# A sum moved behind a turn in neighbourhood attention, and eight copies moved from ScalarE to VectorE

## The chip, the cores and the metric

The kernel runs on one core of a Trainium2 chip. The metric is the device time of one execution, in microseconds. TensorE (PE in the rows) multiplies, VectorE (DVE) and ScalarE (ACT) compute element by element and can read PSUM, GpSimd (POOL) computes on SBUF, and SyncE (SP) issues transfers.

## The reference

Two blocks of a sequence model on 512 tokens of width 1024, all in fp32; the second block has two layers and 256 context tokens beside the 512. The diff touches one part: the attention over a neighbourhood in the even layer. Each of 8 heads of width 64 lets each of 512 queries attend to a window of tokens on a grid and to the 256 context tokens, with a table of biases; the 256 context queries attend to the context alone. The steps that matter, for a block of 128 queries and one head:

```
logits = q @ k.T + bias          # 128 x 256, 384 or 512
p = exp(logits - max(logits))
out = (p / sum(p)) @ v           # 128 x 64
```

## The kernel before, in words

The program is written out by hand for each engine; engines meet by semaphores, and each works off its own list in order. Attention is done in *pairs*: one block of 128 queries for two heads at once. Neighbourhood attention has 24 pairs, six for each of four pairs of heads (`na_pairs`): pairs 0 and 1 of six are the context's queries, which see 256 keys (2 blocks of 128 keys for each head, "short"), pairs 2 to 4 see 512 keys (4 blocks, "wide"), and pair 5 holds the two edges of the grid and sees 384 keys ("edge").

What one pair n goes through:

1. TensorE, `score`: logits of both heads into PSUM (L1083).
2. VectorE, `largest`, once for each head h: takes bias minus logits and its least value (L1193, L1201 for short pairs). It is called M(n,h) below.
3. ScalarE: exponential with its row sum, once for each head (L1161).
4. VectorE: reciprocal of the row sum (L1181); GpSimd: scales the probabilities by it (L1026).
5. TensorE, `turn`: transposes the probabilities into the PSUM banks 6 and 7 (L1101). It waits until they are scaled and until the copy of pair n-1 has emptied the two banks.
6. The copy of the turned probabilities to SBUF (L1149), by ScalarE for all 24 pairs.
7. TensorE, `sum`: probabilities times values (L1121). It waits for the copy.
8. VectorE, `store`: the result to SBUF (L1209).

All pairs of this stage are turned in one piece, the `closing` phase; `phases` says for each piece which engine copies it. The pairs run staggered. At step p of its loop, TensorE turns pair p-3, sums pair p-4 and scores pair p. VectorE's step p holds, in this order: a copy of pair p-3 if it is VectorE's, M(p,0), the reciprocals of pair p-1, the store of pair p-3, M(p,1), and then what `na_between_vector` adds: in steps 0 and 1 of each six the masking of the bias table, in steps 6, 9, 12 and 15 one "mix split" (L1272, a subtraction that prepares the next projection). ScalarE's step for pair p has the first exponential, the copy of pair p-2, the second exponential, and after pairs 5, 8, 11 and 14 a cast for a mix split (L1265). In steps 24 to 26 TensorE has matmuls of the next projection in place of scores.

Attention with grouped queries uses the same class later (stage `gqa`), with other arguments.

Of the kernel before, what the change touches and what calls it, by code (L numbers as in the profile page):

```python
# [19 lines left out]
T = S + CTX  # L20
# [90 lines left out]
class Serial:  # L111
# [3 lines left out]
    def __init__(self, eng, own):  # L115
        self.eng, self.own, self.n, self.at, self.per = eng, own, 0, None, 0
# [351 lines left out]
def wide_products(k, pe, times, bank=7):  # L468

    for _ in range(times):  # L470
        pe.matmul(k.bank(bank), k.h_hi[:, 0, 0:P], k.h_hi[:, 0, 0:S], start=True, stop=True)  # L471
# [173 lines left out]
class Projection:  # L645
# [21 lines left out]
    def tensor(self, pe, lo, ready=None, stored=None, done=0):  # L667
        k, n = self.k, self.tiles
        for i, events in enumerate(self.slots):
            if i < n:  # L670
                u = FIRST[self.name] + i
                size = self.jobs[i][0].shape[-1]
                widths = (S, size - S) if size > S else (S,)
                if i < SPLITS and ready is not None:
                    if i == 0:
                        first_units(k, pe, self.name, k.h_hi, lo, widths, ready)
                else:
                    if i == 1 and stored is not None:
                        pe.wait_ge(*stored)
                    if i >= 3:  # L680
                        pe.wait_ge(self.evac, self.e + i - 2)
                    if u not in HALVED:
                        pe.wait_ge(k.lo_done, u + 1)
                    unit_products(k, pe, 2 * (i % 3), u, k.h_hi, lo, DT, widths, at=(done if i == 0 else 0, DT))
            elif i < n + self.units:
                values_unit(k, pe, self.values, lo, T // P, self.width, i - n, self.units, (self.evac, self.e, n))
            for j in events:
                x, mean = self.jobs[j][0:2]
                size = x.shape[-1]
                pe.wait_ge(self.squares, self.b + j + 1)  # L690
                if j >= 1:
                    pe.wait_ge(self.rooted, self.b + j)
                last = pe.matmul(k.bank(6), mean, k.sq[:, j % 2, 0:S], start=True, stop=True)
                if size > S:
                    last = pe.matmul(k.bank(7, size - S), mean, k.sq[:, j % 2, S:size], start=True, stop=True)
                last.then_inc(self.summed, 1)
# [334 lines left out]
Phase = collections.namedtuple("Phase", "a b by turned kept copies")  # L1031


class RowTiledAttention(PairAttention):


    def __init__(self, k, pairs, third, before, opened, wide=(0, 0, 0), by=("act", "act")):
        super().__init__(k, pairs, third, before, opened, wide)
        count = dict(self.first)
        self.phases, kept = {}, (count["act"], count["dve"])  # L1040
        for p, it in enumerate(pairs):
            n = it["blocks"]
            self.phases[p] = []
            for which, a, b in [(1, 0, 2 * n)] if 2 * n <= TURNED else [(0, 0, n), (1, n, 2 * n)]:
                count["chunks"], count[by[which]] = count["chunks"] + 1, count[by[which]] + 1
                self.phases[p].append(Phase(a, b, by[which], count["chunks"], kept, (count["act"], count["dve"])))
                kept = (count["act"], count["dve"])
        self.last.update(count, pairs=self.last["pairs"], parted=self.last["parted"], mixed=self.last["mixed"], scaled=self.last["scaled"])

# [75 lines left out]
    def tensor(self, pe, begun=0, beside=None):  # L1125
        N = len(self.pairs)
        for p in range(N + 4):
            if p >= 4:
                self.sum(pe, p - 4)
            self.turn(pe, p - 3, self.closing(p - 3))  # L1130
            if begun <= p < N:
                self.score(pe, p)
            if p >= N and beside is not None:
                if p == N:
                    self.place_free(pe)
                beside(p - N)
            if p < 3:
                self.open(pe, "fill", p)
                wide_products(self.k, pe, self.fill[p])
            self.turn(pe, p - 2, self.opening(p - 2))  # L1140
# [513 lines left out]
def attn_views(k):  # L1654

    return (k.view(k.big, 0, 4, T), k.view(k.big, 4 * T, 4, T), k.view(k.big, 8 * T, 6, HALF))
# [7 lines left out]
def pair(q, keys, values, out, bias=None, factor=None):  # L1664

    chunks = [keys[:, a:min(a + CTX, keys.shape[-1])] for a in range(0, keys.shape[-1], CTX)]
    return pair_of([(slice(0, P), q, chunks)], [[(slice(0, P), val)] for val in values], out, bias, factor)


def pair_of(pieces, values, out, bias, factor=None):  # L1670

    return dict(pieces=pieces, ends=list(itertools.accumulate(ap.shape[-1] for ap in pieces[0][2])), n=len(values) * P, values=values,
                blocks=len(values), out=out, bias=bias, factor=factor, joined=factor is not None)
# [29 lines left out]
def na_table(k, t):  # L1703

    return k.view(k.mix_flat, 5 * T, 5, CTX) if t == 0 else k.view(k.big, 12 * T + 5 * CTX * t, 5, CTX)


def na_pairs(k):


    q, key, val = attn_views(k)
    out = []
    for t in range(4):
        vals, mix, table = [val[:, b, t * P:(t + 1) * P] for b in range(6)], k.mix[:, 4 + t, :], na_table(k, t)
        whole, ctx = [[(slice(0, P), v)] for v in vals], key[:, t, S:T]
        for i in (4, 5):
            blk = slice(i * P, (i + 1) * P)
            out.append(pair(q[:, t, blk], ctx, vals[4:], mix[:, blk], bias=[k.par("zero").broadcast_to([P, CTX])] * 2))
        for i in range(3):
            blk = slice(HD + i * P, HD + (i + 1) * P)  # L1720
            out.append(pair_of([(slice(0, P), q[:, t, blk], [key[:, t, i * P:i * P + CTX], ctx])], whole[i:i + 2] + whole[4:],
                               mix[:, blk], bias=[table[:, 0::3, :], table[:, 1:4:2, :]]))
        low, high, units = slice(0, HD), slice(HD, P), table.rearrange("p a (u n) -> p (a u) n", n=P)
        out.append(pair_of([(low, q[:, t, 0:HD], [key[:, t, 0:P], ctx]), (high, q[:, t, S - HD:S], [key[:, t, S - P:S], ctx])],
                           [[(low, vals[0]), (high, vals[3])]] + whole[4:],
                           mix[:, 0:S].rearrange("p (e n) -> p e n", n=HD)[:, ::S // HD - 1, :], bias=[units[:, 4:9:2, :], units[:, 5:10:2, :]]))
    return out
# [59 lines left out]
def gqa_pairs(k):  # L1787

    q, key, val = gqa_views(k)
    return [pair(q[:, t, i * P:(i + 1) * P], key[:, 0, 0:T], [val[:, b, :] for b in range(6)],  # L1790
                 k.mix[:, t, i * P:(i + 1) * P]) for t in range(4) for i in range(4)]


def pair_stages(k):

    first = {("score", 0): [("dil_project_evac", 8), ("values_kept_dve", 1), ("values_kept_act", 1)],
             ("score", 1): [("values_kept_dve", 2), ("values_kept_act", 2)]}
    dil = PairAttention(k, dil_pairs(k), k.big[:, 10240:10240 + 2 * S], None, first, (2, 2, 8))
    first = {("score", 0): [("head_normed", 16), ("values_kept_dve", 5), ("values_kept_act", 4)],
             ("score", 1): [("values_kept_act", 5)]}  # L1800
    diff = PairAttention(k, diff_pairs(k), k.mix_flat[:, 4 * T:6 * T], dil, first, (2, 8, 4))
    first = {("score", 0): [("head_normed", 24), ("head_rooted", 28), ("values_kept_act", 10)],
             ("score", 1): [("values_kept_act", 11)], ("turn", 0): [("head_normed", 28)]}
    na = RowTiledAttention(k, na_pairs(k), k.h_flat[:, 4 * T:6 * T], diff, first, (2, 2, 10))
    first = {("score", 0): [("head_normed", GQA + 2), ("gqa_evac", 5)], ("score", 1): [("gqa_evac", 6)],
             ("fill", 1): [("head_rooted", GQA + 5), ("head_normed", GQA + 5)]}
    first.update({("score", 4 * t): [("head_normed", GQA + 2 + t)] for t in range(1, 4)})
    return dict(dil=dil, diff=diff, na=na, gqa=RowTiledAttention(k, gqa_pairs(k), k.big[:, 4608:4608 + 2 * T], na, first,
                                                                  (0, 8, 4), ("act", "dve")))
# [1845 lines left out]
```

## Time and profile before

| | before |
|---|---|
| time, median of 3 runs | 2461.94 us (2461.26 to 2464.62) |
| time of the profiled execution | 2464.36 us |
| its span | 2462.4 us |
| TensorE busy | 2406.9 us, 98% |
| VectorE busy | 1494.2 us, 61% |
| ScalarE busy | 957.7 us, 39% |
| GpSimd busy | 820.7 us, 33% |
| mean granted TensorE clock | 0.996 |

The span runs from the first to the last instruction of the profiled execution; its time is what was measured for the same execution from outside. The share of busy time is an average over many stages. The stage of the diff lies between about 1086 and 1155 us of the span.

### The profile page before, as it was taken

The numbers are of one execution on the slowest core, as the hardware profiler recorded it, in microseconds if no ns is written. First come the engines' busy times: TensorE is split into PE (matmuls) and PEld (weight loads), VectorE is DVE, ScalarE is ACT, GpSimd is POOL, SyncE is SP. The second block draws the span as 40 slices with busy tenths as digits, with TensorE's granted clock in tenths as the row PEclk, the third lists the DMA queues.
The fourth block names the chain that finished last, engine by engine and source line by source line (L and its number), as shares of the span: only waits on it lengthen the run. The fifth ranks groups of instructions, "written<-read, shape, count | busy, mean of one in ns | idle before, by whom it ended". The sixth has DMA issues, their size and how long they took to land.

```text
span 2462.4 us, 37109 instructions
## 1 busy us (share of the span) xinstructions
PE 2406.9 (98%) x14407; PEld 1965.0 (80%) x14407; DVE 1494.2 (61%) x2060; ACT 957.7 (39%) x1525; POOL 820.7 (33%) x446
## 2 busy tenths in 40 slices
PE   8999999999999999999999999999999999999999
PEld 6778877888886877866888888888878758788887
DVE  6765755457566975685466766644777586424242
ACT  4576644232224545356242222122266322423232
POOL 2533033544441222233223323223224312354443
PEclk9999999999999999999999999999999999999999
DMA  6222023445431110120224434322411111232232
GB/s 250 86 69 78 3 69 120 145 138 187 144 129 37 58 35 20 54 73 2 69 95 137 142 124 137 116 90 94 137 52 51 61 60 60 86 111 94 96 101 85
DMA packets 64663, 227.41 MB, mean 92 GB/s; under 512 B 7041, under 2 KB 9089, under 8 KB 63883
## 3 DMA queue, kind: packets, MB, share of 16 engines
q1 hardware_dynamic: 51160, 176.05, 21.3%
q10 hardware_dynamic: 13362, 49.40, 6.1%
q8 instruction: 99, 1.62, 0.3%
q14 instruction: 42, 0.34, 0.0%
HBM read 223.30 MB, written 2.12 MB: 92 GB/s over the span
## 4 chain that ended last, share of the span: by engine, by line
PE 84%; DVE 7%; issue 4%; ACT 3%; POOL 2%; DMA 0%; SPq 0%; DVEq 0%; POOLq 0%; ACTq 0%
PE ps L277 23%; PE ps L278 23%; PE ps L279 22%; PE ps L1121 2%; POOL w_lo L3172 1%; PE ps L861 1%; PE ps L1083 1%; DVE rstd L760 1%; PE ps L1101 1%; PE ps L878 1%; PE ps L361 1%; PE ps L360 1%; PE ps L359 1%; PE ps L471 1%; PE ps L2944 1%
## 5 line engine op out<-in xcount | busy, mean ns | idle before, releaser
L3172 POOL TENSOR_TENSOR w_lo<-ring,w_hi 128x1024 fp32r<-128x1024 f32 x288 | 702.6, 2440 | 1164.8 <-ACT w_hi L270 661.7
L277 PE MATMUL ps<-act_hi,w_hi 128*128 128x512 f32 x2280 | 843.2, 370 | 8.1 <-DVE act_lo_mixer L592 5.7
L279 PE MATMUL ps<-act_hi,w_lo 128*128 128x512 f32 x2280 | 829.4, 364 | 0.0
L278 PE MATMUL ps<-act_lo_ffn,w_hi 128*128 128x512 f32 (+1 forms) x1408 | 512.8, 364 | 0.0
L277 PEld LDWEIGHTS ps<-act_hi,w_hi 128*128 128x128 f32 x2280 | 429.7, 188 | 97.6 <-issue 17.7
L279 PEld LDWEIGHTS ps<-act_hi,w_lo 128*128 128x128 f32 x2280 | 428.6, 188 | 71.9
L270 ACT CAST w_hi<-ring 128x1024 fp32r<-128x1024 f32 (+1 forms) x167 | 172.6, 1034 | 654.7 <-PE ps L279 605.6
L1494 ACT CAST w_hi<-ring 128x1024 fp32r<-128x1024 f32 (+1 forms) x132 | 137.6, 1043 | 458.2 <-PE ps L279 458.2
L1386 DVE SCALAR_TENSOR_TENSOR ada_place<-ada_place 128x1024 f32<-128x1024 f32 x180 | 285.0, 1583 | 24.5 <-DMA ada_place<-in_w_ada 10.2
L278 PEld LDWEIGHTS ps<-act_lo_ffn,w_hi 128*128 128x128 f32 x1408 | 265.1, 188 | 41.0
L277 PE MATMUL ps<-hidden_hi,w_hi 128*128 128x512 f32 x704 | 256.4, 364 | 1.8 <-DVE hidden_lo L1577 1.5
L278 PE MATMUL ps<-hidden_lo,w_hi 128*128 128x512 f32 x704 | 256.5, 364 | 0.0
L279 PE MATMUL ps<-hidden_hi,w_lo 128*128 128x512 f32 x704 | 255.3, 363 | 0.0
L1577 DVE TENSOR_TENSOR hidden_lo<-probs,hidden_hi 128x512 f32 (+3 forms) x66 | 149.2, 2260 | 64.2 <-ACT hidden_hi L1520 64.2
L1575 DVE TENSOR_TENSOR probs<-probs,ps 128x512 f32<-128x512 f32 (+1 forms) x66 | 51.2, 776 | 210.0 <-PE ps L279 202.3
L277 PEld LDWEIGHTS ps<-hidden_hi,w_hi 128*128 128x128 f32 x704 | 132.6, 188 | 25.1 <-DVE hidden_lo L1577 2.4
L279 PEld LDWEIGHTS ps<-hidden_hi,w_lo 128*128 128x128 f32 x704 | 132.3, 188 | 21.8
L278 PEld LDWEIGHTS ps<-hidden_lo,w_hi 128*128 128x128 f32 x704 | 132.6, 188 | 20.5
L278 PE MATMUL ps<-act_lo_mixer,w_hi 128*128 128x512 f32 (+1 forms) x416 | 148.0, 356 | 0.0
L760 DVE RECIPROCAL rstd<-probs 128x768 f32<-128x768 f32 x20 | 99.0, 4950 | 41.8 <-ACT probs L737 41.7
L1562 DVE SCALAR_TENSOR_TENSOR probs<-ps,params,probs 128x511 f32<-128x511 f32 x66 | 43.6, 661 | 132.4 <-ACT probs L1509 131.6
L1614 DVE SCALAR_TENSOR_TENSOR x_res<-ps,mod,x_res 128x512 f32<-128x512 f32 x72 | 47.6, 662 | 124.3 <-PE ps L279 123.1
(445 smaller groups left out, 3224.5 us busy)
## 6 DMA issues: line engine op xcount, KB each, us to landing
ring<-in_w_ffn SPq DMA_DIRECT2D x204, 512.0 KB, 3.2
ada_place<-in_w_ada ACTq DMA_DIRECT2D x90, 512.0 KB, 4.2
ring<-in_w_gdn SPq DMA_DIRECT2D x16, 512.0 KB, 3.2
ring<-in_w_hy SPq DMA_DIRECT2D x12, 512.0 KB, 3.2
ring<-in_w_dil_qk SPq DMA_DIRECT2D x8, 512.0 KB, 8.7
ring<-in_w_out SPq DMA_DIRECT2D x8, 512.0 KB, 3.3
ring<-in_w_diff_qk SPq DMA_DIRECT2D x8, 512.0 KB, 3.3
ring<-in_w_na_qk SPq DMA_DIRECT2D x8, 512.0 KB, 3.2
```

Source lines behind the costliest of these rows:

```text
L270: s.eng.copy(k.w_hi[:, u % SPLITS, rest], k.ring[:, u % SLOTS, rest]).then_inc(k.hi_done, 1)
L277: pe.matmul(out, w[0], x[0], start=start, stop=False)
L278: pe.matmul(out, w[0], x[1], start=False, stop=False)
L279: return pe.matmul(out, w[1], x[0], start=False, stop=stop)
L760: link(v, v.eng.reciprocal(k.rstd[:, 0:size], k.probs[:, j % 2, 0:size]))
L1121: last = pe.matmul(k.ps[r, out + cols.start:out + cols.stop], v[:, r], self.probs_turned(p, g, g + 1)[:, cols], start=b == 0 and cols.star ...
L1386: ins = v.eng.scalar_tensor_tensor(k.ada[:, 4, :], k.ada[:, 2 + n % 2, :], 1.0, k.ada[:, q, :], ALU.mult, ALU.mult, accum_out=k.mod_flat[: ...
L1494: s.eng.copy(k.w_hi[:, (u + j) % SPLITS, rest], k.ring[:, (u + j + 2) % SLOTS, rest]).then_inc(k.hi_done, 1)
L1575: v.eng.tensor_tensor(tmp[:, 0:n], tmp[:, 0:n], k.ps[:, val:val + n], ALU.mult).then_inc(f.hidden, 1)
L1577: v.eng.tensor_tensor(k.hid_lo[:, it * 2 + a, 0:n], tmp[:, 0:n], k.hid_hi[:, it * 2 + a, 0:n].bitcast(F32), ALU.subtract).then_inc(f.ready, 1)
L1614: ins = v.eng.scalar_tensor_tensor(k.x[:, j, a:b], k.ps[:, buf + a:buf + b], k.mod[:, f.layer, 40 + j, q:q + 1], k.x[:, j, a:b], ALU.mult, ...
L3172: pool.tensor_tensor(k.w_lo[:, a % SPLITS, :], k.ring[:, a % SLOTS, :], k.w_hi[:, a % SPLITS, :].bitcast(F32), ALU.subtract).then_inc(k.lo ...
```

## The change

Two arguments are added to `RowTiledAttention`, and both are given for the neighbourhood attention alone. `turn_first` puts the turn of pair p-3 ahead of the sum of pair p-4 in each step of TensorE's loop. `short="dve"` gives the copy of a pair with at most two blocks of keys for a head to VectorE: 8 of 24 pairs here. The stage `gqa` has six blocks in every pair and keeps its order and its engines.

```diff
-    def __init__(self, k, pairs, third, before, opened, wide=(0, 0, 0), by=("act", "act")):
+    def __init__(self, k, pairs, third, before, opened, wide=(0, 0, 0), by=("act", "act"), turn_first=False, short="act"):
         super().__init__(k, pairs, third, before, opened, wide)
+        self.turn_first = turn_first
...
-                count["chunks"], count[by[which]] = count["chunks"] + 1, count[by[which]] + 1
-                self.phases[p].append(Phase(a, b, by[which], count["chunks"], kept, (count["act"], count["dve"])))
+                engine = short if n <= 2 else by[which]
+                count["chunks"], count[engine] = count["chunks"] + 1, count[engine] + 1
+                self.phases[p].append(Phase(a, b, engine, count["chunks"], kept, (count["act"], count["dve"])))
...
     def tensor(self, pe, begun=0, beside=None):
         N = len(self.pairs)
         for p in range(N + 4):
+            if self.turn_first:
+                self.turn(pe, p - 3, self.closing(p - 3))
             if p >= 4:
                 self.sum(pe, p - 4)
-            self.turn(pe, p - 3, self.closing(p - 3))
+            if not self.turn_first:
+                self.turn(pe, p - 3, self.closing(p - 3))
             if begun <= p < N:
                 self.score(pe, p)
...
-    na = RowTiledAttention(k, na_pairs(k), k.h_flat[:, 4 * T:6 * T], diff, first, (2, 2, 10))
+    na = RowTiledAttention(k, na_pairs(k), k.h_flat[:, 4 * T:6 * T], diff, first, (2, 2, 10), turn_first=True, short="dve")
```

In the changed kernel the lines of the turn, the scores and the sum are L1103, L1085 and L1123 (before: L1101, L1083, L1121), those of the copy, the maxima and the store L1154, L1198, L1206 and L1214 (before: L1149, L1193, L1201 and L1209), and that of the mix split L1277 (before: L1272).

TensorE's list around a short pair, steps 8 to 10, before. `ps` is PSUM; `probs`, `pair_probs` and `act_place` are the three places of probabilities, here those of pairs 6, 7 and 5; `big` holds queries, keys and values.

```order
L1121 MATMUL ps<-pair_turned,big 64x128 x8
L1101 MATMUL ps<-consts,act_place 128x64 x12
L1083 MATMUL ps<-big 128x256 x4
L1121 MATMUL ps<-pair_turned,big 64x64 x4
L1121 MATMUL ps<-pair_turned,big 64x128 x4
L1101 MATMUL ps<-consts,probs 128x64 x8
L1083 MATMUL ps<-big 128x256 x4
L1121 MATMUL ps<-pair_turned,big 64x128 x4
L1101 MATMUL ps<-consts,pair_probs 128x64 x8
L1083 MATMUL ps<-big 128x256 x4
```

The same steps now:

```order
L1103 MATMUL ps<-consts,act_place 128x64 x12
L1123 MATMUL ps<-pair_turned,big 64x128 x8
L1085 MATMUL ps<-big 128x256 x4
L1103 MATMUL ps<-consts,probs 128x64 x8
L1123 MATMUL ps<-pair_turned,big 64x64 x4
L1123 MATMUL ps<-pair_turned,big 64x128 x4
L1085 MATMUL ps<-big 128x256 x4
L1103 MATMUL ps<-consts,pair_probs 128x64 x8
L1123 MATMUL ps<-pair_turned,big 64x128 x4
L1085 MATMUL ps<-big 128x256 x4
```

The turns of pairs 5, 6 and 7 have each moved ahead of the sum of the pair before.

VectorE's list from the second maximum of pair 8 to the first of pair 10, before. The `ISA` rows are the maxima, each followed by the reading of its accumulator.

```order
L1193 ISA act_place,small<-ps,big 128x512
L1193 ISA small 128x1
L1193 ISA probs,small<-ps,big 128x512
L1193 ISA small 128x1
L1181 RECIPROCAL small<-small 128x1 x2
L1209 COPY mix<-ps 128x128
L1193 ISA probs,small<-ps,big 128x512
L1193 ISA small 128x1
L1272 TENSOR_TENSOR mix_lo<-mix,act_hi 128x768
L1193 ISA pair_probs,small<-ps,big 128x512
```

The same part now:

```order
L1198 ISA act_place,small<-ps,big 128x512
L1198 ISA small 128x1
L1154 COPY pair_turned<-ps 128x2x4x64
L1198 ISA probs,small<-ps,big 128x512
L1198 ISA small 128x1
L1186 RECIPROCAL small<-small 128x1 x2
L1214 COPY mix<-ps 128x128
L1198 ISA probs,small<-ps,big 128x512
L1198 ISA small 128x1
L1277 TENSOR_TENSOR mix_lo<-mix,act_hi 128x768
L1154 COPY pair_turned<-ps 128x2x4x64
L1198 ISA pair_probs,small<-ps,big 128x512
```

The two rows of L1154 are new: the copies of pairs 6 and 7, each behind the second maximum of the step before, the latter behind the mix split too.

## Rows read from the trace of the kernel before

The columns of a timeline are the start, the duration, the engine, the line, the operation, what it writes and reads, and in brackets how long the engine stood idle before it and what ended that. The columns of a stretch are its length, then the busy time and the instructions of TensorE's matmuls, its weight loads, VectorE, ScalarE and GpSimd, then the granted clock, the share of the DMA engines and GB/s.

**Rows 1.** Page of the profiled execution, part 1: TensorE's busy time, share of the span, instructions.

```profile
PE 2406.9 (98%) x14407; PEld 1965.0 (80%) x14407; DVE 1494.2 (61%) x2060; ACT 957.7 (39%) x1525; POOL 820.7 (33%) x446
```

**Rows 2.** Busy time by engine over four stretches, each from the turn of pair 6k.

```profile
1091.39:1106.76 15.37, 13.18 (x205) 9.62 (x206) 11.13 (x48) 13.45 (x32) 7.17 (x12) 1.00 0.37 151
1106.76:1122.82 16.06, 13.24 (x207) 9.55 (x206) 12.18 (x50) 13.78 (x33) 7.18 (x12) 1.00 0.01 2
1122.82:1138.77 15.95, 13.24 (x206) 9.56 (x205) 11.21 (x49) 12.65 (x31) 7.19 (x12) 1.00 0.01 3
1138.77:1145.85 7.08, 6.48 (x98) 4.54 (x96) 5.23 (x25) 6.79 (x16) 4.26 (x7) 1.00 0.01 3
```

**Rows 3.** TensorE's waits from 1091.39 to 1145.85: total, times, longest.

```profile
PE ps L1121 <- ACT pair_turned L1149: 8.1, 13, 1.3
```

**Rows 4.** Timeline, steps 18 and 19: start, duration, engine, line.

```profile
1129.75 1.09 PE L1121 MATMUL ps<-pair_turned,big 128*64 128x128 f32 x16 [1.25 <-ACT pair_turned L1149]
...
1130.78 0.71 PE L1101 MATMUL ps<-consts,probs 64*128 64x64 f32 x16
...
1130.89 0.29 DVE L1209 COPY mix<-ps 128x128 f32<-128x128 f32 x1 [0.28 <-PE ps L1121]
...
1131.32 0.65 PE L1083 MATMUL ps<-big 64*128 64x256 f32 x4
...
1131.53 1.01 ACT L1149 COPY pair_turned<-ps 128x1024 f32<-128x1024 f32 x1 [0.52 <-PE ps L1101]
...
1132.59 1.09 PE L1121 MATMUL ps<-pair_turned,big 128*64 128x128 f32 x16 [0.62 <-ACT pair_turned L1149]
```

**Rows 5.** Timeline, steps 15 to 17, around the short pairs 12 and 13.

```profile
1121.99 0.90 PE L1121 MATMUL ps<-pair_turned,big 128*64 128x64 f32 x16
...
1122.93 0.29 DVE L1209 COPY mix<-ps 128x128 f32<-128x128 f32 x1
...
1123.13 0.68 DVE L1193 CUSTOM_DVE_ANT_1 act_place<-ps,big 128x512 f32<-128x512 f32 x1
...
1124.39 0.66 PE L1121 MATMUL ps<-pair_turned,big 128*64 128x128 f32 x8 [0.20 <-ACT pair_turned L1149]
...
1125.12 1.36 POOL L1026 TENSOR_SCALAR act_place<-act_place,small 128x512 f32<-128x512 f32 x2 [1.15 <-DVE small L1181]
...
1125.17 0.27 DVE L1209 COPY mix<-ps 128x128 f32<-128x128 f32 x1
...
1125.97 1.32 DVE L1272 TENSOR_TENSOR mix_lo<-mix,act_hi 128x768 fp32r<-128x768 f32 x1
...
1126.97 0.72 PE L1101 MATMUL ps<-consts,act_place 64*128 64x64 f32 x16
...
1127.21 0.68 DVE L1193 CUSTOM_DVE_ANT_1 pair_probs<-ps,big 128x512 f32<-128x512 f32 x1
...
1128.71 0.99 ACT L1149 COPY pair_turned<-ps 128x1024 f32<-128x1024 f32 x1
```

**Rows 6.** Copies of 128x512 out of PSUM, VectorE's and ScalarE's: times run, busy, mean ns.

```profile
L996 DVE COPY pair_turned<-ps 128x512 f32<-128x512 f32 x4 | 2.8, 691 | 1.6 <-PE ps L878 1.6
...
L1149 ACT COPY pair_turned<-ps 128x512 f32<-128x512 f32 x8 | 4.5, 564 | 0.0
```

**Rows 7.** Timeline, the start of the stage, and around pairs 11 to 13.

```profile
1091.73 0.67 DVE L1193 CUSTOM_DVE_ANT_1 act_place<-ps,mix 128x512 f32<-128x512 f32 x1
...
1114.26 0.82 ACT L1265 CAST act_hi<-mix 128x768 fp32r<-128x768 f32 x1
...
1117.99 0.41 DVE L1201 CUSTOM_DVE_ANT_0 probs<-ps,params 128x256 f32<-128x256 f32 x1
...
1119.11 0.96 DVE L1272 TENSOR_TENSOR mix_lo<-mix,act_hi 128x768 fp32r<-128x768 f32 x1
...
1119.99 0.41 DVE L1201 CUSTOM_DVE_ANT_0 pair_probs<-ps,params 128x256 f32<-128x256 f32 x1
...
1121.14 0.80 ACT L1149 COPY pair_turned<-ps 128x768 f32<-128x768 f32 x1
```

## The prediction

> **What bounds the kernel now.** First the page: TensorE is busy for 98% of the span [rows 1]. A matmul's end is modelled there, so this says only that the engine is hardly ever without work: time that TensorE stands still in one stage is not made up in another. Next, how much it stands still in the stage that the diff touches. Take the 24 pairs from the turn of pair 0 (1091.39 us) to the turn of pair 21 (1145.85 us): 54.46 us in the four stretches of [rows 2], with TensorE busy for 46.14 of them, and of the rest 8.1 us in 13 waits of a sum (L1121) for ScalarE's copy L1149 [rows 3]. ScalarE is busy for 46.67 us, VectorE for 39.75 us. Three engines are thus at 73 to 86%, and what counts is the loop through them. The timeline shows it for wide pairs [rows 4]: sum 14 at 1129.75, turn 15 at 1130.78, copy 15 at 1131.53 for 1.01 us, sum 15 at 1132.59, so 2.84 us a step, in series sum, turn, copy; only the scores of 0.65 us lie beside the copy. VectorE's store comes 1.14 us after its sum starts, and right behind it the second head's bias-and-maximum.
>
> I write T(n), S(n), C(n) for turn, sum, scores of pair n, M(n,h) for VectorE's maximum of head h, and k for the group of six pairs.
>
> **What the reordering gives.** Both T(n) and S(n-1) wait for copy n-1. With T first, copy n starts a sum earlier, and S(n-1) and C(n+3) run beside it. For a wide pair the step is then no longer 1.03 + 0.75 + 1.06 = 2.84 us, but TensorE's own work: 0.71 + 1.09 + 0.65 = 2.45 less a little overlap, 2.4 us. That is a gain of some 0.4 us on each wide step on which nothing else is late, and nothing on the last three steps (24 to 26), where TensorE has the next projection beside the pairs and hardly waits.
>
> **What is late next.** In VectorE's program M(n,1) stands behind the store of pair n-3, which needs S(n-3), and S(n-3) now stands behind T(n-2). So M(n,1) comes later against the turns than before. That is harmless while ScalarE copies. But the new VectorE copy of a short pair stands, as the order shows, behind exactly this M. Before T(6k+1) can start, this has to happen one after the other:
> - T(6k), eight transposes: half of the 0.71 us of sixteen and a release, 0.42 us;
> - S(6k-1) to its store, 0.94 us (1121.99 to 1122.93 in [rows 5]);
> - store to M(6k+2,1), 0.20 us, and M itself, 0.68 us [rows 5];
> - the copy on VectorE, 0.69 us, where ScalarE took 0.56 us [rows 6], and 0.05 us until TensorE goes on (1132.54 to 1132.59 in [rows 4]).
>
> That is 2.98 us, where S(11) to S(12) took 2.40 [rows 5]. From T(6k+1) to T(6k+2) the same with the short sum (1124.39 to 1125.17, 0.78 us): 2.82 us, where TensorE alone would need about 2.1. In steps 9 and 15 VectorE has in addition a mix split (L1272) between M and the copy. Its rows show 0.96 us (1119.11 in [rows 7]) and 1.32 us at 1125.97, where it lies partly beside GpSimd's scaling from 1125.12 on [rows 5]. In the new order the scaling is nearly over when the split begins, so I take 1.0: 3.82 us for this step. (The Trainium skill, SBUF — State Buffer, Who interferes with whom, says that a VectorE instruction with two SBUF inputs contends with a GpSimd instruction that reads SBUF; the two durations agree with it. By that rule with full overlap both splits would take 1.32 us and the sum would be 0.6 us more.)
>
> The other steps, from the same rows:
> - T(6k+2) to T(6k+3): M(6k+4,0) starts as the VectorE copy ends, then as at 1127.21 (M), 1128.71 (copy of the wide pair, behind the first exponential), 1129.75 (TensorE goes on) [rows 4, 5]: 1.50 + 1.04, less the 0.05: 2.49 us.
> - T(6k+3) to T(6k+4): TensorE's own 2.4 us. In two of the groups ScalarE has a cast of 0.82 us (1114.26 in [rows 7]) ahead of the exponential and copy, of which I count 0.7 as not hidden: 3.1 us.
> - T(6k+4) to T(6k+6): turn to sum 0.72, sum to store 1.14, store to M 0.21, M(12,1) to M(13,0) 2.00 with the split between them (1117.99 to 1119.99), on to the copy 1.15 (1121.14), copy to TensorE 0.85 [rows 5, 7]: 6.07 us. Without the split, 0.88 less: 5.19 us.
>
> **The sum**, against the stretches of [rows 2]:
> - pairs 0 to 6: at the start nothing is stored yet, so T(1) waits only for M(2,1) at 1091.73 [rows 7] and the copy: 0.34 + 0.68 + 0.74 = 1.76; then 2.82 + 2.49 + 3.1 + 6.07. In all 16.24 against 15.37: +0.87.
> - pairs 6 to 12, both splits and the cast: 2.98 + 3.82 + 2.49 + 3.1 + 6.07 = 18.46 against 16.06: +2.40.
> - pairs 12 to 18: 2.98 + 3.82 + 2.49 + 2.4 + 5.19 = 16.88 against 15.95: +0.93.
> - pairs 18 to 21: 2.98 + 2.82 + 2.49 = 8.29 against 7.08: +1.21.
>
> Together +5.4 us. At T(21) the new order has also one sum more still to do, S(20), 1.0 us on an engine that is full from there on. So +6.4 us at the end of the stage. The rest of the program is untouched and bound by TensorE, so all of it arrives. The profiled execution has a span of 2462.4 us and a time of 2464.36 us; its 2464.36 is 2.4 above the median of the three runs, 2461.94, to which I add the 6.4: 2468.3 us (2470.8 would be the same for that one execution). ScalarE's relief, eight copies of 0.56 us, is worth nothing in this sum: in the short steps it waits for maxima, not TensorE for it.
>
> **Rivals.**
> 1. Faster: the maxima and copies on VectorE keep up, and TensorE's own work sets every step. The short steps would have to come down from 2.98 and 2.82 us to about 2.2, so it holds only if M and copy together take under 0.8 us where the rows have 0.68 + 0.74. For it speaks that VectorE is idle for 27% of the stage. All of the 8.1 us of [rows 3] would be the bound, 2453.8 us. With 2.4 us for wide steps, 2.1 to 2.6 for the others, three groups of 14.0, 6.9 for the last stretch and the 1.0 of S(20) make 49.9 against 54.46: -4.6 us, 2457.4 us. Chance 0.10, of which 0.06 beyond the bound of measurement.
> 2. Given back: my short steps stand, but half of the waits of 3.1 and 6.07 us is hidden, since ScalarE and VectorE do them in moments in which they would wait anyway. Then the sum is between +1 and +4.9: about 2465 us. Chance 0.25.
> 3. Worse: T(n) waits for GpSimd's scaling, which it now needs a sum earlier. Before, the scaling of pair 14 that starts at 1125.12 ends at 1126.48, and its turn starts at 1126.97 [rows 5], half a microsecond later. In my walk the VectorE copy delays the turn by more than this, so I see no wait; but up to 0.5 us on six to eight steps would add 3 to 4 us: 2471.5 us. Chance 0.12.
>
> The forecast itself has 0.53, with a range of its own of 2466.8 to 2470 us: the seven short turns of 0.42 us at 0.3 or 0.5 give -0.8 or +0.6, the two splits at 0.96 or 1.32 nothing or +0.6, the two casts at 0.4 or 0.8 -0.6 or +0.2.
>
> **How the numbers follow.** A measurement of this kernel tells 0.2%, 4.9 us, from no change. Slower beyond it: the forecast but for 0.01, and rival 3: 0.64. Within it: rival 2, 0.04 of rival 1 and 0.01 of the forecast: 0.30. Faster beyond it: 0.06. The range leaves out rival 1 and the mild end of rival 2 below, and the far end of rival 3 above: 2461.5 to 2472 us.
>
> **What the new profile would show.** Eight VectorE copies of 128x512 of about 0.69 us in the stage, each starting as an M of 0.68 us ends and not when its turn ends. TensorE's waits before turns, not before sums, and the longest of them, over 1.5 us, on VectorE's copies of pairs 7 and 13. From the turn of pair 0 to that of pair 21 about 60 us; wide steps of 2.4 us where no split or cast lies. It is wrong if short steps come out under 2.5 us, if ScalarE's copies of wide pairs no longer end a wait at all, or if turns wait for GpSimd.

## The result

| | before | after |
|---|---|---|
| time, median of 12 runs | 2460.93 us (2457.94 to 2464.62) | 2465.93 us (2464.58 to 2467.92) |
| ratio to before, 95% interval | | 1.0019 (1.0012 to 1.0027) |
| time of the profiled execution | 2464.36 us | 2465.30 us |
| its span | 2462.4 us | 2463.3 us |
| turn of pair 0 to turn of pair 21 | 54.46 us | 58.16 us |
| turn of pair 0 to start of the last sum | 62.09 us | 66.92 us |

The change makes the kernel slower by 5.0 us between the medians and by 0.19% (4.7 us) in the ratio, just at the 0.2% that were taken as the bound of "no change", and clear of 1 in its interval. The last row is the one that answers for it: +4.83 us, all in the stage of the diff. The spans of the two profiled executions differ by 0.9 us only, because what lies behind the last sum, untouched by the diff, took 1308.92 us in the one and 1306.62 in the other, and what lies ahead of turn 0 1.6 us less. One profile's span therefore can't tell 5 us of 2460 here; a stage can.

These differences outside the stage go with TensorE's clock. Ahead of the stage and behind it there are short stretches in which the granted clock is at the lower of its two levels, 1.2 GHz instead of 2.4: 20.5 us in all in the profiled execution before, 14.9 in the one after. In the stage itself it is at the upper level, here and in every run below. Such a stretch in the kernel before, with as much ahead of it and behind it (length; busy time of TensorE, its weight loads, VectorE, ScalarE and GpSimd; then the granted clock):

```profile
1214.70:1221.50 6.80, 6.52 (x43) 5.58 (x42) 1.23 (x2) 2.49 (x3) 1.65 (x1) 1.00 0.23 77
1221.50:1228.30 6.80, 6.80 (x26) 5.92 (x26) 1.49 (x4) 1.16 (x3) 0.71 (x1) 0.50 0.24 77
1228.30:1235.10 6.80, 6.60 (x30) 4.51 (x28) 6.57 (x13) 4.44 (x8) 0.00 (x0) 1.00 0.00 0
```

TensorE was busy for 6.52 of the 6.80 us before the clock fell. Over the kernels below, the part behind the stage is shortest in the two with the least time at the lower level (runs 1 and 9, 1304.4 us) and longest in the three with the most (before, runs 6 and 8, 1308.7 to 1308.9). The whole times show it too. Of the 95 executions of the kernel before that were timed beside the runs below, 45 have a mean clock of 0.998 and a median of 2458.70 us, 25 have 0.997 and 2461.81, 18 have 0.996 and 2464.46. The changed kernel has 2464.82 us at 0.998 (3 executions) and 2466.53 at 0.997 (8). A straight line through the 95 gives, as an estimate, 2.3 us for each 0.001 of mean clock, and the changed kernel's 12 executions lie on average 4.8 us above it: the +4.83 of the stage.

The page of the profile after, part 1, answers to [rows 1]:

```profile
PE 2407.1 (98%) x14407; PEld 1965.1 (80%) x14407; DVE 1498.9 (61%) x2068; ACT 956.2 (39%) x1517; POOL 821.6 (33%) x446
```

VectorE has 8 instructions and 4.7 us more, ScalarE 8 fewer and 1.5 us less (957.7 before): the copies have moved, though the totals over the whole span don't show the 4.5 us of [rows 6] one to one. TensorE's busy time is the same to 0.2 us. Where the time went is seen in the four stretches from turn 6k to turn 6k+6, with the columns of [rows 2]:

```profile
1089.76:1105.60 15.84, 12.81 (x188) 9.52 (x189) 11.60 (x48) 11.92 (x28) 7.39 (x12) 1.00 0.32 131
1105.60:1123.52 17.92, 13.79 (x205) 10.21 (x205) 12.83 (x50) 13.04 (x31) 7.39 (x12) 1.00 0.00 1
1123.52:1139.83 16.31, 13.85 (x204) 10.15 (x205) 11.57 (x48) 12.41 (x30) 7.13 (x12) 1.00 0.01 3
1139.83:1147.92 8.09, 6.58 (x98) 4.60 (x97) 6.40 (x25) 5.47 (x14) 3.67 (x6) 1.00 0.01 3
```

They were forecast at 16.24, 18.46, 16.88 and 8.29 us. The one with a cast and both mix splits grew most, by 1.9 us; the last, without any, grew by 1.0 in three steps. TensorE's waits from turn 0 to turn 21, which were [rows 3] before:

```profile
PE ps L1103 <- DVE pair_turned L1154: 6.5, 8, 1.5
PE ps L1103 <- issue: 2.5, 6, 0.7
PE ps L1103 <- POOL probs L1026: 2.1, 2, 1.1
```

Sums no longer wait; turns do, and the list is headed by VectorE's copy, 8 times, 6.5 us. Here is the timeline from the turn of pair 6 to that of pair 8:

```profile
1105.60 0.47 PE L1103 MATMUL ps<-consts,probs 64*128 64x64 f32 x8 [1.07 <-POOL probs L1026]
...
1106.00 0.90 PE L1123 MATMUL ps<-pair_turned,big 128*64 128x64 f32 x16
...
1106.94 0.29 DVE L1214 COPY mix<-ps 128x128 f32<-128x128 f32 x1 [0.73 <-PE ps L1123]
1107.14 0.68 DVE L1198 CUSTOM_DVE_ANT_1 act_place<-ps,big 128x512 f32<-128x512 f32 x1
...
1107.75 0.69 DVE L1154 COPY pair_turned<-ps 128x512 f32<-128x512 f32 x1
...
1108.35 0.68 DVE L1198 CUSTOM_DVE_ANT_1 probs<-ps,big 128x512 f32<-128x512 f32 x1
...
1108.58 0.47 PE L1103 MATMUL ps<-consts,pair_probs 64*128 64x64 f32 x8 [0.62 <-DVE pair_turned L1154]
...
1109.68 0.29 DVE L1214 COPY mix<-ps 128x128 f32<-128x128 f32 x1 [0.50 <-PE ps L1123]
...
1109.89 0.68 DVE L1198 CUSTOM_DVE_ANT_1 probs<-ps,big 128x512 f32<-128x512 f32 x1
...
1110.49 0.95 DVE L1277 TENSOR_TENSOR mix_lo<-mix,act_hi 128x768 fp32r<-128x768 f32 x1
...
1111.37 0.68 DVE L1154 COPY pair_turned<-ps 128x512 f32<-128x512 f32 x1
...
1112.19 0.71 PE L1103 MATMUL ps<-consts,act_place 64*128 64x64 f32 x16 [1.50 <-DVE pair_turned L1154]
```

Read it downwards. Turn 6 at 1105.60 is followed by sum 5 at 1106.00; its store at 1106.94 had kept VectorE waiting for 0.73 us; then comes the second maximum of pair 8, and only then the copy of pair 6, at 1107.75. Turn 6 is only 0.47 us long, so its result had lain ready for 1.7 us. Turn 7 starts at 1108.58, 2.98 us after turn 6. The next round is the same with a mix split of 0.95 us in it, 3.61 us. The eight copies themselves, by form:

```profile
L1154 DVE COPY pair_turned<-ps 128x512 f32<-128x512 f32 x8 | 5.5, 687 | 0.0
```

### The profile page after: what moved, and what is told of

It reads as the page before. It is cut to its first block, busy times and chain, and to the rows that moved or that the text cites. A ratio compares the mean times of both kernels' runs of the same rounds, so it can differ in the third digit from the quotient of the medians.

```text
span 2463.3 us, 37109 instructions
## 1 busy us (share of the span) xinstructions
PE 2407.1 (98%) x14407; PEld 1965.1 (80%) x14407; DVE 1498.9 (61%) x2068; ACT 956.2 (39%) x1517; POOL 821.6 (33%) x446
## 4 chain that ended last, share of the span: by engine, by line
PE 84%; DVE 7%; issue 4%; ACT 2%; POOL 2%; DMA 0%; SPq 0%; DVEq 0%; POOLq 0%; ACTq 0%
PE ps L277 23%; PE ps L278 23%; PE ps L279 22%; PE ps L1123 2%; POOL w_lo L3177 1%; PE ps L1085 1%; PE ps L1103 1%; PE ps L861 1%; DVE rstd L760 1%; PE ps L878 1%; PE ps L359 1%; PE ps L361 1%; PE ps L360 1%; PE ps L471 1%; PE ps L2949 1%
```

## The experiments

"Stage" is the time from the start of turn 0 to the start of sum 23 in the profiled execution. "At equal clock" is an estimate: how far the executions of a kernel lie on average above the straight line through the 95 executions of the kernel before (section on the result), each taken at its own mean clock.

| run | turn first | short copies | other edit | ratio (95%) | at equal clock, us | stage, us | stage to before |
|---|---|---|---|---|---|---|---|---|
| before | no | ScalarE | | 1 | 0 | 62.09 |  |
| after | yes | VectorE | | 1.0019 (1.0012 to 1.0027) | +4.8 | 66.92 | +4.83 |
| 1 | yes | ScalarE | | 1.0006 (0.9997 to 1.0015) | +0.9 | 63.26 | +1.17 |
| 2 | no | VectorE | | 1.0015 (1.0006 to 1.0024) | +2.1 | 64.16 | +2.07 |
| 3 | yes | VectorE | store behind the maximum | 1.0000 (0.9991 to 1.0009) | +0.3 | 62.76 | +0.67 |
| 4 | yes | VectorE | copy ahead of the store | 1.0012 (1.0003 to 1.0021) | +2.2 | 64.03 | +1.94 |
| 5 | yes | VectorE | splits in the wait | 1.0014 (1.0005 to 1.0023) | +2.4 | 64.46 | +2.37 |
| 6 | yes | ScalarE | splits in the wait | 1.0002 (0.9993 to 1.0011) | -0.7 | 61.33 | -0.76 |
| 7 | yes | ScalarE | store last | 0.9994 (0.9985 to 1.0003) | -2.0 | 60.28 | -1.81 |
| 8 | no | ScalarE | store last | 1.0001 (0.9992 to 1.0010) | -0.8 | 61.26 | -0.83 |
| 9 | yes | ScalarE | store last, splits and casts moved | 0.9990 (0.9981 to 0.9998) | -2.9 | 59.46 | -2.63 |
| 10 | yes | VectorE | as run 9 | 0.9991 (0.9982 to 1.0000) | -3.5 | 59.15 | -2.94 |
| 11 | yes | ScalarE | run 7 once more | 0.9994 (0.9986 to 1.0003) | -2.1 | 60.26 | -1.83 |

Runs 7 and 11 are the same kernel and give 60.28 and 60.26 us of stage, where the whole program scatters over some 6 us. In all twelve rows the estimate at equal clock agrees with the stage to 0.6 us, in ten of them to 0.3.

### 1 and 2: one part of the change alone

```diff
-    na = RowTiledAttention(..., first, (2, 2, 10), turn_first=True, short="dve")
+    na = RowTiledAttention(..., first, (2, 2, 10), turn_first=True)   # run 1
+    na = RowTiledAttention(..., first, (2, 2, 10), short="dve")       # run 2
```

> The turn goes ahead of the sum, and ScalarE copies all 24 pairs as before. Theory A (the cost comes from short copies that stand on VectorE behind a maximum, which waits for the sum that was moved back): the short steps fall to 2.3 and 2.1 us, wide ones to 2.3 or 3.1, and from the turn of pair 0 to that of pair 21 it takes about 53 us against 54.46 before and 58.16 in the changed kernel; with the 1.1 us of the sum that is left over, no difference from before, -1.5 to +0.5 us. Rival B (the order alone costs it, since all second maxima come a turn later): 57 us or more in that stretch and at least +3 us.

> VectorE copies the short pairs, and the sum stays ahead of the turn. Theory A: from sum to sum the short steps are 0.94 + 0.20 + 0.68 + 0.74 = 2.56 and 2.40 us (3.28 with a mix split), against 2.40 and 1.99 before, and the step after them 2.49 us: about +0.5 us for each of four short couples, +2 us in all, so the two parts alone add up to clearly less than the +5 us of both. Rival B: the copies on VectorE cost nothing by themselves, 0 to +0.5 us. Rival C (the copies carry the whole loss): +4 to +5 us.

The stage is 1.17 us longer than before with the turn alone, and 2.07 us with the copies alone. Together that is 3.2 us of the 4.8: 1.6 us come only from having both, as theory A says; rival B of run 1 and rivals B and C of run 2 are out by the stage. By the ratios the parts are +1.5 and +3.7 us with intervals of 4 to 5 us, which does not tell a sum from an interaction. At equal clock they are +0.9 and +2.1, 1.8 us short of both together, which bears the stages out.

The turn alone takes 54.61 us from turn 0 to turn 21 where I expected 53, about what it was before (54.46); the other 1.0 us of its stage is the sum left over at turn 21. Its timeline from the split of step 9 on:

```profile
1111.22 1.11 DVE L1277 TENSOR_TENSOR mix_lo<-mix,act_hi 128x768 fp32r<-128x768 f32 x1
...
1112.26 0.68 DVE L1198 CUSTOM_DVE_ANT_1 pair_probs<-ps,big 128x512 f32<-128x512 f32 x1
...
1113.04 0.72 ACT L1166 ACTIVATE pair_probs<-pair_probs,small 128x512 f32<-128x512 f32 x1 [0.88 <-DVE small L1198]
...
1113.76 0.99 ACT L1154 COPY pair_turned<-ps 128x1024 f32<-128x1024 f32 x1
...
1114.85 0.71 PE L1103 MATMUL ps<-consts,probs 64*128 64x64 f32 x16 [1.16 <-POOL probs L1026]
```

Before, the same split made one step of 3.81 us; here it makes one of 3.26 (turn 8 at 1111.59 to turn 9 at 1114.85). That is the gain. But the split of step 12, which in the old order lay in slack (2.31 us from turn 11 to 12), now makes that step 3.69 us. The second group of six pairs thus takes 16.79 us (16.06 before) and gives back what the third, whose only split stands in step 15, gains: 15.24 (15.95 before). The list of waits names GpSimd's scaling for turn 9. The rows show another: the copy of pair 8 ends at 1114.75, 0.10 us ahead of the turn, and this copy stands on ScalarE behind the exponential that waited for VectorE's maximum at 1112.26.

With the copies alone, VectorE at the same place:

```profile
1109.23 0.69 DVE L1154 COPY pair_turned<-ps 128x512 f32<-128x512 f32 x1
...
1110.92 0.68 DVE L1198 CUSTOM_DVE_ANT_1 probs<-ps,big 128x512 f32<-128x512 f32 x1
...
1111.53 1.33 DVE L1277 TENSOR_TENSOR mix_lo<-mix,act_hi 128x768 fp32r<-128x768 f32 x1
1112.78 0.68 DVE L1154 COPY pair_turned<-ps 128x512 f32<-128x512 f32 x1
```

And the two sums on TensorE that wait for the copies:

```profile
1110.02 0.66 PE L1123 MATMUL ps<-pair_turned,big 128*64 128x128 f32 x8 [0.33 <-issue]
...
1113.56 0.66 PE L1123 MATMUL ps<-pair_turned,big 128*64 128x128 f32 x8 [1.57 <-issue]
```

The copy at 1112.78 stands behind the split of 1.33 us, and sum 7 starts at 1113.56, 3.54 us after sum 6 (1.99 before).

### 3 and 4: take the maximum, or the sum too, from ahead of the copy

```diff
 # run 3
-            late = p < N and self.pairs[p]["bias"] is None
+            late = p < N
 # run 4
-            self.copy(v.eng, "dve", v.eng.tensor_copy, p - 3, self.closing(p - 3))
+            if not self.turn_first:
+                self.copy(v.eng, "dve", v.eng.tensor_copy, p - 3, self.closing(p - 3))
...
                 invert(p - 1, 1)
+            if self.turn_first:
+                self.copy(v.eng, "dve", v.eng.tensor_copy, p - 2, self.closing(p - 2))
```

> The changed kernel with one edit: in VectorE's steps the store stands behind the second maximum and not ahead of it (a sum is awaited only then). The maximum of 0.68 us thus leaves the path from turn to copy, but the copy still waits for the sum by way of the store. Theory A: short steps of 2.3 and 2.15 us instead of 2.98 and 2.8 (3.0 with a split instead of 3.6), the two steps before pair 6k 4.75 to 5 us instead of 5.0 and 5.9: 6 to 7 us less than the changed kernel, so 1 to 2 us faster than before. Rival (the length of the copy and of the turns themselves makes the short steps): they stay above 2.7 us, and at most 2 us are gained.

> The changed kernel with one edit: VectorE's copy of pair p-2 stands in step p behind the reciprocals and ahead of the store and the second maximum, so that it waits for its turn alone. Theory A: the short steps fall to what TensorE needs, 2.3 and 2.1 us, also beside a mix split, which then delays only a later exponential by up to 0.9 us; 4 to 5 us less than the changed kernel, about level with before. Rival (VectorE, which then waits for a turn before its store and maximum, passes the wait on): the short steps are at or below 2.4 us but the wide ones grow, and it stays 3 us or more above before.

Run 3, turns 6, 7 and 8:

```profile
1106.53 0.46 PE L1103 MATMUL ps<-consts,probs 64*128 64x64 f32 x8 [0.73 <-POOL probs L1026]
...
1108.90 0.46 PE L1103 MATMUL ps<-consts,pair_probs 64*128 64x64 f32 x8
...
1112.21 0.71 PE L1103 MATMUL ps<-consts,act_place 64*128 64x64 f32 x16 [1.19 <-DVE pair_turned L1154]
```

The short steps are 2.37 and 3.31 us, against 2.98 and 3.61: the maximum is off the path. The stage is 4.16 us shorter than in the changed kernel, and the time 5 us, back to that of before. I had expected 6 to 7 us; the two steps ahead of pairs 6 and 12 stayed at 5.55 us instead of 5.0. Not M(6k,1) held them there, but the store that waits for its sum, with the split behind it: with the store behind the split too, in run 7, they take 5.0 us.

Run 4:

```profile
1107.06 0.46 PE L1103 MATMUL ps<-consts,probs 64*128 64x64 f32 x8 [1.07 <-POOL probs L1026]
...
1109.25 0.41 PE L1103 MATMUL ps<-consts,pair_probs 64*128 64x64 f32 x8
...
1111.75 0.71 PE L1103 MATMUL ps<-consts,act_place 64*128 64x64 f32 x16 [0.44 <-POOL act_place L1026]
```

The first short step is TensorE's own 2.19 us, the second, beside the split, 2.50. But the next is 3.36 instead of 2.37. The three together take 8.05 us (8.96 in the changed kernel, 7.96 before): the split costs its time one step later, and the rival's point, that VectorE passes its wait on, holds for half of the gain. The stage is 2.9 us shorter than in the changed kernel, between the 4 to 5 of theory A and the rival's 1.8 or less.

### 5 and 6: put the mix splits into VectorE's wait

```diff
+            if waiting is not None:
+                waiting(p)
             if p >= 3 and not late:
                 store(p - 3)
...
-    if p in (6, 9, 12, 15):
-        mix_split_vector(k, v, "mix_e", T, ((p - 6) // 3,), (p - 6) // 3)
...
+def na_waiting_vector(k, v, p):
+    if p in (7, 10, 13, 16):
+        mix_split_vector(k, v, "mix_e", T, ((p - 7) // 3,), (p - 7) // 3)
```

> The changed kernel with one edit: VectorE's four mix splits of 0.95 us stand in the next step ahead of the store (steps 7, 10, 13, 16), where VectorE waits 0.5 to 1.1 us for a sum in the changed kernel, and no longer ahead of a short copy or of the first maximum that releases ScalarE. Theory A (what stands on VectorE between sum and copy is on the path): the short step of 3.61 us falls to 2.75 to 2.85, the two steps of 5.9 us ahead of pairs 6 and 12 to about 5.1, so 3 us less in the stage from turn 0 to sum 23 (66.92 in the changed kernel): about 64, +2 us against before. Rival (the splits cost the same wherever they stand, since VectorE is full): less than 1 us gained.

> The turn first, ScalarE copying all pairs (as in the run with the turn alone), and the mix splits in VectorE's wait ahead of the store. Theory A: the steps of 3.26 and 5.9 us there fall to 2.5 and 5.1; stage 60 to 61 us against 62.09 before and 63.26 with the turn alone, time 1 to 2 us below before. Rival B (with the turn first, GpSimd's scaling, for which six turns seemed to wait 5.6 us, sets the steps): the stage stays at 62 us or more, since the scaling does not come earlier.

Both stages fall, by 2.46 us (expected 3) and by 1.93 us (expected 2.3 to 3.3). In run 5 the step of 3.61 us is 2.74, as expected, and the two steps ahead of pair 12 take 5.40 us instead of 5.90 (expected 5.1). So the same instruction costs differently by where it stands, and theory A holds; it expected somewhat more, since it left out what the split still delays behind it. Run 6 also puts rival B out, which had the stage at 62 us or more. By the ratio run 5 is 3.4 us above before (1.2 to 5.7), with 2.4 at equal clock.

### 7, 8 and 11: the store last

```diff
-            late = p < N and self.pairs[p]["bias"] is None
-            if p >= 3 and not late:
-                store(p - 3)
             if p < N:
                 largest(p, 1)
-            if p >= 3 and late:
-                store(p - 3)
             if between is not None:
                 between(p)
+            if p >= 3:
+                store(p - 3)
```

> The turn first, ScalarE copying all pairs, and VectorE's store as the last thing of its step, behind the second maximum, the masking and the mix split, so that nothing but the next step's first maximum waits for a sum. Theory A: the second maxima come 0.5 to 1 us earlier and the splits fall into the wait; steps near TensorE's own 2.1 to 2.6 us; stage about 60 us, 2 us below before. Rival: the next first maximum now waits for the sum, its exponential stands ahead of ScalarE's copy, and the stage stays at 62 to 63 us.

> The kernel before with the store as the last thing of VectorE's step, no turn first and no copy on VectorE. It tells whether what the run before it may gain needs the turn first at all. Theory A: in the old order the wide step is sum, turn, copy in series (2.84 us), which no order on VectorE shortens; only the steps with a split gain (3.81 to about 3.3, twice): stage 61 us, -1 us. Rival: it gains as much as the same edit with the turn first, -2 us or more.

> The run with the turn first and the store last once more, beside the two others on one chip: again 0 to 2 us below before, stage 60.3 us. If it is not, differences of this size between calls are those of the measurement.

With the turn first the stage is 60.28 us, 1.8 below before; with the old order it is 61.26, 0.8 below. So the turn first is worth 1.0 us once the second maxima don't wait for the sum: the reordering is good for a little, and VectorE's order had hidden it. No ratio is clear of 1 by its interval, and that of run 8, 1.0001, does not show its gain; at equal clock runs 7, 11 and 8 are at -2.0, -2.1 and -0.8 us. GpSimd's scaling in run 7, by tile (shortest, median, longest):

```profile
L1026 POOL TENSOR_SCALAR act_place<-act_place,small x2: 695/1040/1386, 1109.5 to 1110.1; 128x512 f32<-128x512 f32 x2
L1026 POOL TENSOR_SCALAR probs<-probs,small x2: 695/696/696, 1111.9 to 1112.6; 128x512 f32<-128x512 f32 x2
```

One scaling of 128x512 took 1386 ns, the other three 695: it ran beside the mix split of 1.02 us, and turn 8 had to wait for it (2.97 us from turn 7). This is rival 3 of the prediction, found in another kernel. The split had started first, at 1109.94, the scaling at 1110.14, and the scaling paid 0.69 us. At 1125.97 in [rows 5] the second scaling had started first, at 1125.78, and it was VectorE's split that grew, to 1.32 us, while the two scalings took 1.36. (The Trainium skill, SBUF — State Buffer, Who interferes with whom: "Issue order, not op shape, decides who blocks." The trace agrees in both places.)

### 9 and 10: the version that follows

```diff
-    if p in (5, 8, 11, 14):                    # ScalarE's casts
+    if p in (7, 10, 13, 16):
...
-    if p in (6, 9, 12, 15):                    # VectorE's mix splits
+    if p in (11, 12, 17, 18):
```

> The run with the turn first and the store last, with the casts and mix splits put where the trace of that run shows the engines waiting: ScalarE's casts after pairs 7, 10, 13, 16 (it waited 1.2 us there), VectorE's splits in steps 11, 12, 17, 18, so that none stands ahead of the maxima and beside the scaling of a wide pair that the next turn needs (2.06 us for a scaling that takes 1.36 elsewhere). Theory A: the steps of 2.97 us fall to 2.3, those of 2.94 with a cast to 2.4; the stage takes 58 to 59 us against 60.28 there and 62.09 before, time 3 to 4 us (0.15%) below before. Rival (the engines are too full for the 0.8 to 0.95 us pieces to hide anywhere): stage 60 us or more, within 2 us of before.

> The same with VectorE copying the short pairs. It tells what that part of the change costs where nothing but a sum and a store stand between turn and copy: 0.42 + 0.94 + 0.20 + 0.74 = 2.3 us and 2.1 us for the short steps, about what TensorE needs. Theory A: 0 to 1 us above the run without it. Rival (the copies cost 2 us wherever they stand, as they did alone): 2 us or more above.

Run 9's stage is 59.46 us, 2.6 below before (expected 3 to 4, with the rival at 2 or less); its ratio of 0.9990 (0.9981 to 0.9998) is the only one that is clear of no change on the fast side. Run 10 has the whole change in it, turn first and VectorE's copies, and its stage is 59.15 us. The copies of pairs 12 and 13 in run 10:

```profile
1121.37 0.29 DVE L1214 COPY mix<-ps 128x128 f32<-128x128 f32 x1
1121.57 0.68 DVE L1154 COPY pair_turned<-ps 128x512 f32<-128x512 f32 x1
...
1122.40 0.46 PE L1103 MATMUL ps<-consts,pair_probs 64*128 64x64 f32 x8
...
1123.79 0.28 DVE L1214 COPY mix<-ps 128x128 f32<-128x128 f32 x1
1123.99 0.68 DVE L1154 COPY pair_turned<-ps 128x512 f32<-128x512 f32 x1
...
1124.82 0.71 PE L1103 MATMUL ps<-consts,act_place 64*128 64x64 f32 x16 [0.30 <-DVE pair_turned L1154]
```

Only the store (1121.37, 1123.79) stands ahead of each copy, and each turn follows 2.4 us after the one before. The stage is 0.3 us below that of run 9 (expected 0 to 1 above; the rival, 2 or more above, is out). Both parts of the change are harmless here, and 7.8 us of stage lie between this kernel and the changed one, which differ in the order of one engine's small instructions and the places of eight casts and splits.

## Why the prediction was right

It was right in direction and in mechanism, and the time lies in the range that it gave, 2461.5 to 2472 us. In size it was too high: 2468.3 us against 2465.93, or +6.4 us against +5.0 between the medians and +4.8 in the stage. One of the 2.4 us between the times comes from the median before, 2461.94 us over three executions and 2460.93 over twelve. The result also lies below the forecast's own narrower range, 2466.8 to 2470 us, and the most likely case, slower beyond 0.2%, stands at its edge.

- *Both orders wait for the same copy, so the turn first takes the sum out of the wide loop.* Shown: 2.32 us from turn 15 to 16 where neither cast nor split lies, against 2.4 forecast and 2.84 before. With a cast 3.06 (3.1 forecast).
- *The second maximum waits for a later sum, and the short copy stands behind it.* Shown by the rows above, and by run 3, which moves the store behind the second maxima and takes away 4.16 of the 4.83 us, 3.3 of them in the eight short steps.
- *The terms.* Turn 6k to 6k+1: 2.98 forecast, 2.98 measured, though this is luck in part, as two errors cancel. Next: 2.82 and 2.75; with a split 3.82 and 3.61. Next: 2.49 and 2.37. The two steps ahead of pair 6k: 6.07 and 5.90, without a split 5.19 and 5.03. The sum left over at turn 21: 1.0 and 1.13. All but the first and the last measured less than forecast. Three things make the differences. An instruction on VectorE starts 0.60 us after one whose row says 0.69 (1107.75 to 1108.35 in the changed kernel), so chains of back-to-back rows are shorter than their sum. From the start of VectorE's copy to the turn it takes 0.83 us (1107.75 to 1108.58), not 0.69 + 0.05: the 0.05 was read at a sum behind ScalarE's copy. In the first term these two cancel, 0.07 us each way. And from the maximum of pair 13 to the copy of pair 11 it took 1.03 us (below), not 1.15, since in the old trace that copy had waited for its turn. In all the walk gave +6.4 and the stage has +4.83: the sum of these terms was mis-sized by 1.6 us, and with it the forecast "slower beyond 0.2%" stands at 0.19%.
- *ScalarE's relief is worth nothing.* Not shown apart from the cost of VectorE's copies. Run 2, which gives the same relief without the new order, is slower by 2.07 us of stage; run 10 against run 9 is faster by 0.31, so some gain remains where VectorE's copies are early.
- *Rival 1, faster to 2457.4.* Out. Its condition, maximum and copy under 0.8 us, is about what run 10 gives by taking the maximum away (and by moving casts and splits), and there the stage is 2.9 us below before.
- *Rival 2, half given back.* By its number, between +1 and +4.9 us and about 2465 us, it is as near to the result as the forecast; the range alone doesn't tell them apart. Its reason is out: casts and splits were not hidden by half (3.06 of 3.1, 5.90 of 6.07), and the 1.6 us are spread over all the terms.
- *Rival 3, turns waiting for GpSimd.* Not in this kernel, though the waits name it for 2.1 us. The rows at turn 12:

```profile
1121.61 0.42 DVE L1206 CUSTOM_DVE_ANT_0 pair_probs<-ps,params 128x256 f32<-128x256 f32 x1
...
1122.21 1.18 POOL L1026 TENSOR_SCALAR probs<-probs,small 128x256 f32<-128x256 f32 x2 [3.20 <-DVE small L1186]
...
1122.64 0.78 ACT L1154 COPY pair_turned<-ps 128x768 f32<-128x768 f32 x1
...
1123.52 0.46 PE L1103 MATMUL ps<-consts,probs 64*128 64x64 f32 x8 [1.07 <-POOL probs L1026]
```

The scaling ends at 1123.39 and ScalarE's copy at 1123.42; turn 12 needs both. Both hang on VectorE, which does the maximum at 1121.61 and the reciprocals behind it after the split. The gaps tell which came last, if narrowly: where a scaling is the last of the two, the turn starts 0.05 us after its end (turns 2, 8, 14 and 20 of run 1, turn 8 of run 7), and behind a copy of ScalarE 0.10 us after (turn 9 of run 1 above). Turn 12 starts 0.10 us after the copy; for the scaling alone it could have started 0.08 us earlier. No run took the two apart.
- *The signs of being wrong.* No short step is under 2.5 us, and no turn waits for GpSimd beyond the copy. The third sign was that ScalarE's copies of wide pairs no longer end a wait, and the list of waits indeed names none. The rows do:

```profile
1115.11 1.37 POOL L1026 TENSOR_SCALAR pair_probs<-pair_probs,small 128x512 f32<-128x512 f32 x2 [0.92 <-DVE small L1186]
...
1116.53 0.99 ACT L1154 COPY pair_turned<-ps 128x1024 f32<-128x1024 f32 x1
...
1117.62 0.72 PE L1103 MATMUL ps<-consts,pair_probs 64*128 64x64 f32 x16 [0.69 <-issue]
```

Turn 10 stood idle for 0.69 us and starts 0.10 us after the copy of pair 9, while its scalings had ended 1.1 us before. The list puts this wait down to "issue". The stretch from turn 0 to turn 21 was forecast at about 60 us and took 58.16.

The times of runs 2 and 5 exceed their stages by more than 1 us (+3.7 and +3.4 by the ratios, +2.1 and +2.4 in the stage). Their executions had a lower mean clock than those of the kernel before beside them (0.9968 and 0.9969 against 0.9974 both times), and at equal clock they are at +2.1 and +2.4. What stays open is why the number of stretches at the lower level differs from execution to execution.

## What to carry to other kernels

When a step is moved back on one engine, look at what another engine has queued behind the instruction that waits for it: the sum that went one turn later held a store, the store a maximum, and the maximum a copy that had been put on that engine by the same change. Each part was cheap; the order between them was not. Where an engine must wait, put its waiting instruction last in its step and the filler ahead of it, and judge such edits by the length of the stage, which came within 0.02 us in the one kernel that was run twice, and not by whole times that scatter by 6, unless they are compared at equal clock.

## What the runs showed of the hardware

- Two 128x512 copies out of PSUM to the same tile, one on each engine: 687 ns on VectorE, 564 on ScalarE [rows 6]. The next instruction on VectorE starts 0.60 us after such a copy's start, TensorE's turn 0.83 us after, which is 0.14 to 0.15 us after its end; behind a copy of ScalarE it is 0.10 us.
- A scaling on GpSimd and a two-input subtraction on VectorE, both SBUF to SBUF, lengthen one another, and which one pays changes: 695 to 1386 ns for the scaling in run 7, where the subtraction had started first, and 0.95 to 1.33 us for the subtraction in run 2, where the scaling had (1111.36 against 1111.53).
- TensorE's granted clock was at its upper level in the stage of every run, and at the lower one for 20.5 us elsewhere in the span before and 14.9 in the one after. The slices of the page show "9" all the same, which is 90% or more. The 6 us by which whole times scatter go with it: 2458.70 us at a mean clock of 0.998, 2464.46 at 0.996.
